# A decoder layer on eight cores: fused layer norms, a reordered retention slot, value weights loaded behind x, and a final wait for the stores alone

## The reference

```python
def layer_norm(x, w, b):
    mu = mean(x); var = mean((x - mu)**2)
    return (x - mu) * rsqrt(var + 1e-5) * w + b

hcat = x @ w_in                                  # 1024 -> 3584 columns
b_gate, c_gate, hc, q, k, v, g = split(hcat)     # 512 each
y_conv = b_gate * causal_short_conv(c_gate * hc, conv_w)    # 3 taps, per channel
q = rotary(q, positions)
k = rotary(k, positions) * 128 ** -0.5           # 4 heads of 128
o = chunkwise_retention(q, k, v)                 # chunks of 128 rows, decay per head
y_ret = silu(g) * head_group_norm(o, ret_gn_w, ret_gn_b)
mix = concat([y_conv, y_ret]) @ w_out
x = layer_norm(ALPHA * x + mix, ln1_w, ln1_b)
ff = relu(x @ w_ff1) ** 2 @ w_ff2                # 1024 -> 4096 -> 1024
ple = sigmoid(x @ w_ple_gate) * (p @ w_ple_proj)
x = layer_norm(ALPHA * x + ff + ple, ln2_w, ln2_b)
```

## Time and profile before

| what | value |
|---|---|
| median of 6 runs | 859.25 us (856.6 to 929.13) |
| profiled execution, its own time | 856.81 us |
| its span on the slowest core (core 2) | 855.3 us |
| spans of the eight cores | 850.6 to 855.3 us |
| TensorE busy | 804.4 us, 94% of the span |
| VectorE busy | 444.1 us, 52% |
| ScalarE busy | 271.5 us, 32% |
| GpSimd busy | 154.0 us, 18% |
| HBM read and written | 194.19 and 18.87 MB, 249 GB/s over the span |

### The profile page before, as it was taken

How to read it: one execution, slowest core, us unless ns; L and a number is a source line. 1 busy time by engine, 2 the same in 40 slices (tenths; PEclk the granted TensorE clock), 3 DMA queues, 4 the chain that set the end, 5 groups by cost and what they waited for, 6 DMA issues and landing times.

```text
span 855.3 us, 12652 instructions; the slowest of 8 cores (850.6 to 855.3 us)
## 1 busy us (share of the span) xinstructions
PE 804.4 (94%) x4088; PEld 375.1 (44%) x4088; DVE 444.1 (52%) x700; ACT 271.5 (32%) x496; POOL 154.0 (18%) x213
## 2 busy tenths in 40 slices
PE   3899999999979899999999999999999999999992
PEld 1344444444545344444444444444444444444441
DVE  4268745546675343635286453538555336845253
ACT  2132225554566533113144302324330222431000
POOL 7000025553455300010011000101100000100000
PEclk9999999999999999999999999999999999999996
DMA  9999999524219699999779946567976565776111
GB/s 127 219 170 156 107 168 158 88 51 99 51 19 166 164 189 195 171 174 197 185 179 243 239 122 156 140 154 215 202 217 151 146 148 170 173 204 140 52 50 49
DMA packets 22575, 128.41 MB, mean 150 GB/s; under 512 B 2864, under 2 KB 4016, under 8 KB 11056
## 3 DMA queue, kind: packets, MB, share of 16 engines
q0 software_dynamic: 13008, 81.27, 55.8%
q1 hardware_dynamic: 8928, 45.30, 15.3%
q10 hardware_dynamic: 576, 1.05, 0.3%
HBM read 194.19 MB, written 18.87 MB: 249 GB/s over the span
## 4 chain that ended last, share of the span: by engine, by line
PE 75%; DMA 8%; DVE 5%; issue 4%; POOL 4%; ACT 3%; DVEq 0%; ACTq 0%; POOLq 0%
PE ps L194 73%; DMA wc_61<-wc 4%; DMA ring_106<-w_ff 4%; ACT sqj L223 2%; PE psT L198 2%; POOL st_51 L201 1%; DVE ra_80 L201 1%; DVE ob_93 L201 1%; DVE PT_90 L201 1%; DVE ob_94 L201 0%; DVE xacc_119 L201 0%; ACT xacc_119 L223 0%; DVE PT_89 L201 0%; DVE lnst L696 0%; POOL xT_56 L236 0%
## 5 line engine op out<-in xcount | busy, mean ns | idle before, releaser
L201 DVE TENSOR_TENSOR hT<-ps,tR_129 128x512 bf16<-128x512 f32 x43 | 29.6, 688 | 30.9 <-ACT tR_129 L223 30.7
L201 POOL TENSOR_TENSOR lnst<-lnst,neghalf 128x1 f32<-128x1 f32 x32 | 19.4, 607 | 133.9 <-DVE lnst L205 133.9
L201 DVE TENSOR_TENSOR hT<-ps,tR_130 128x512 bf16<-128x512 f32 x42 | 28.9, 688 | 27.4 <-ACT tR_130 L223 27.3
L201 DVE TENSOR_TENSOR hT<-ps,tR_128 128x512 bf16<-128x512 f32 x43 | 29.6, 688 | 25.8 <-ACT tR_128 L223 25.0
L223 ACT ACTIVATE tR_128<-ps 128x512 f32<-128x512 f32 x43 | 25.7, 597 | 53.5 <-PE ps L194 49.7
L223 ACT ACTIVATE tR_129<-ps 128x512 f32<-128x512 f32 x43 | 25.6, 596 | 53.0 <-PE ps L194 47.6
L223 ACT ACTIVATE tR_130<-ps 128x512 f32<-128x512 f32 x42 | 25.1, 597 | 52.5 <-PE ps L194 51.2
L201 DVE TENSOR_TENSOR xacc_120<-ps,xacc_120 128x512 f32<-128x512 f32 x16 | 11.1, 692 | 52.1 <-PE ps L194 52.0
L194 PE MATMUL ps<-ring_110,hT 128*128 128x512 bf16 x160 | 36.2, 379 | 0.0
L194 PE MATMUL ps<-ycat,ring_106 128*128 128x512 bf16 x160 | 35.8, 379 | 0.2 <-DMA ring_106<-w_ff 0.2
L194 PE MATMUL ps<-ring_108,hT 128*128 128x512 bf16 x160 | 36.0, 379 | 0.0
(11 more groups left out here) (277 smaller groups left out, 1540.0 us busy)
## 6 DMA issues: line engine op xcount, KB each, us to landing
s_ff<-w_ff POOLq DMA_DIRECT2D x8, 1024.0 KB, 43.8
ring_106<-w_ff POOLq DMA_DIRECT2D x6, 1024.0 KB, 20.3
ring_105<-w_ff POOLq DMA_DIRECT2D x6, 1024.0 KB, 10.0
ring_110<-w_ff POOLq DMA_DIRECT2D x6, 1024.0 KB, 10.9
ring_108<-w_ff POOLq DMA_DIRECT2D x6, 1024.0 KB, 11.0
ring_109<-w_ff POOLq DMA_DIRECT2D x6, 1024.0 KB, 15.4
ring_107<-w_ff POOLq DMA_DIRECT2D x5, 1024.0 KB, 10.7
ring_104<-w_ff POOLq DMA_DIRECT2D x5, 1024.0 KB, 9.5
```

Of the source, the lines that this page charges most:

```text
L201: self.P.op(eng, lambda e: e.tensor_tensor(out=out, in0=in0, in1=in1, op=op), reads, writes)
```

## The change

The final wait of all engines for everything becomes one wait on sp for the stores (`join`). The layer norm loses its ScalarE pass and its bias step: two fused VectorE passes compute (x - mean) x weight and then x rstd + bias; epsilon is added in the same step as the aggregate, and rstd has a name of its own, so that only the second pass waits for the power. `x1_cast` is taken out of `gen_ln1` and placed by hand. In a retention slot the scores move from behind `do_rot(t, 1)` to ahead of `do_y`; in slots 9 to 12 three background steps and `do_norm` come ahead of `do_v`; slot 17 gets one more `ff1_group` ahead of `do_y`. wVf waits for xT[3] instead of wc[1]. Unit (1,0) runs alone and by piece, the units after it in a new order, and `center_v` enters after unit (2,2). ff1 makes one background step per group instead of two.

```diff
--- before.py
+++ after.py
@@ -99,21 +99,8 @@
     def dma(self, eng, fn, sem_key, reads=(), writes=()):
         return self._add(eng, fn, reads, writes, is_dma=True, sem_key=sem_key)
 
-    def join_all(self):
-        last = {}
-        dmas = {}
-        for o in self.ops:
-            if o.fn is not None:
-                last[o.eng] = o.idx
-                if o.is_dma:
-                    dmas[o.sem_key] = o.idx
-        for e in ENGS:
-            o = self._add(e, None, [], [])
-            for le, li in last.items():
-                if le != e:
-                    o.deps.setdefault(li, True)
-            for li in dmas.values():
-                o.deps.setdefault(li, True)
+    def join(self, eng, reads):
+        self._add(eng, None, reads, [])
 
     def emit(self, stack, tag):
         nc = self.nc
@@ -432,7 +419,7 @@
         for i, (t, n) in enumerate(((wG, "wG"), (wQ, "wQ"), (wK, "wK"))):
             cast(t[:], wqkvg[i], n, n)
         h.dma("sp", wVf[:], wqkvg[3].rearrange("p a (h e) -> p (a h) e", e=128), "wVf",
-              wc_res[1], ["wVf"])
+              xT_res[3], ["wVf"])
 
         wsrc = dict(wout=(w_out, s_wout), ff1=(w_ff1, s_ff1), gate=(w_gate, s_gate),
                     ff2=(w_ff2, s_ff2))
@@ -557,13 +544,12 @@
 
         conv((0, 0), by_piece=True)
         conv((0, 1), by_piece=True)
-        conv((1, 0), (1, 1), by_piece=True)
-        for tt, j in ((0, 2), (1, 2), (0, 3), (1, 3)):
+        conv((1, 0), by_piece=True)
+        for tt, j in ((1, 1), (0, 2), (1, 2), (0, 3), (1, 3), (2, 0), (2, 1), (2, 2)):
             conv((tt, j))
         bg.add(center_v())
-        for tt in (2, 3):
-            for j in range(4):
-                conv((tt, j))
+        for tt, j in ((2, 3), (3, 0), (3, 1), (3, 2), (3, 3)):
+            conv((tt, j))
         bg.flush()
         issue_casts(4)
         prefetch(3)
@@ -690,26 +676,20 @@
             st6 = lnst[:, slot, 0:12]
             mv = lnst[:, slot, 12:14]
             rstd = lnst[:, slot, 14:15]
-            nbias = lnst[:, slot, 15:16]
-            rl = ("lnst", slot)
+            rl, rr = ("lnst", slot), ("rstd", slot)
             for hf in range(2):
                 P.op("dve", lambda e, hf=hf: e.bn_stats(out=st6[:, hf * 6:(hf + 1) * 6],
                                                         in_=buf[:, hf * 512:(hf + 1) * 512]),
                      [rbuf], [rl])
                 yield
             P.op("dve", lambda e: e.bn_aggr(out=mv, in_=st6), [rl], [rl])
+            h.ts("dve", rstd, mv[:, 1:2], LN_EPS, ALU.add, [rl], [rr])
             yield
-            h.ts("dve", rstd, mv[:, 1:2], LN_EPS, ALU.add, [rl], [rl])
+            h.tt("pool", rstd, rstd, neghalf[:, 0:1], ALU.pow, [rr, "neghalf"], [rr])
             yield
-            h.tt("pool", rstd, rstd, neghalf[:, 0:1], ALU.pow, [rl, "neghalf"], [rl])
+            h.stt(buf, buf, mv[:, 0:1], w_t[:], ALU.subtract, ALU.mult, [rbuf, rl, rw], [rbuf])
             yield
-            h.stt(nbias, mv[:, 0:1], -1.0, rstd, ALU.mult, ALU.mult, [rl], [rl])
-            yield
-            h.act(buf, buf, AF.Identity, [rbuf, rl], [rbuf], scale=rstd, bias=nbias)
-            yield
-            h.tt("dve", buf, buf, w_t[:], ALU.mult, [rbuf, rw], [rbuf])
-            yield
-            h.tt("dve", buf, buf, b_t[:], ALU.add, [rbuf, rb], [rbuf])
+            h.stt(buf, buf, rstd, b_t[:], ALU.mult, ALU.add, [rbuf, rr, rb], [rbuf])
             yield
 
         def load_xin(k):
@@ -745,8 +725,9 @@
 
         def gen_ln1(tt, bi):
             yield from gen_ln(x1v(tt, bi), x1r(tt, bi), lnt[0], lnt[1], "ln1w", "ln1b", bi)
+
+        def x1_cast(tt, bi):
             h.cp("act", x1b[bi % 2][:], x1v(tt, bi), [x1r(tt, bi)], [("x1b", bi % 2)])
-            yield
 
         def x1_transpose(tt, bi):
             b = tt * 4 + bi
@@ -777,21 +758,32 @@
         slabs0 = []
         chains = []
         for t in range(NB + 2):
+            norm_first = 9 <= t <= 12
+            if norm_first:
+                bg.step(3)
+                do_norm(t - 2)
             if t < NB:
                 do_v(t)
             elif t == NB:
                 ff1_group(0, next_bank())
             bg.step()
-            if 0 <= t - 2 < NB:
+            if 0 <= t - 2 < NB and not norm_first:
                 do_norm(t - 2)
             if 0 <= t - 1 < NB:
                 do_qkT(t - 1)
+            if 10 <= t < 14:
+                bg.until(chains[t - 10])
+                x1_cast(0, t - 10)
             bg.step()
             if t < NB:
                 do_rot(t, 0)
             else:
                 ff1_group(0, next_bank())
+            if 0 <= t - 1 < NB:
+                do_scores(t - 1)
             bg.step()
+            if t > NB:
+                ff1_group(0, next_bank())
             if 0 <= t - 2 < NB:
                 do_y(t - 2)
             bg.step()
@@ -799,17 +791,13 @@
                 do_rot(t, 1)
             elif t == NB:
                 ff1_group(0, next_bank())
-            bg.step()
-            if 0 <= t - 1 < NB:
-                do_scores(t - 1)
-            bg.step()
+            bg.step(2)
             if t + 2 < NB:
                 do_g(t + 2)
             elif t <= NB:
                 ff1_group(0, next_bank())
             bg.step()
             if 10 <= t < 14:
-                bg.until(chains[t - 10])
                 x1_transpose(0, t - 10)
             if 0 <= t - 1 < NB:
                 do_o(t - 1)
@@ -852,7 +840,7 @@
         def phase_ff1(tt):
             while ff1["n"] < 32 * (tt + 1):
                 ff1_group(tt, bank3())
-                bg.step(2)
+                bg.step()
 
         scnt = [0]
 
@@ -886,6 +874,8 @@
         def gen_norm1(tt):
             for bi in range(4):
                 yield from gen_ln1(tt, bi)
+                x1_cast(tt, bi)
+                yield
                 yield
                 yield
                 x1_transpose(tt, bi)
@@ -952,13 +942,17 @@
                       [r, ("rstd", bi), "ln2b"], [r])
                 h.dma(("sp", "act")[k], out[b * 128:(b + 1) * 128, k * 512:(k + 1) * 512], v,
                       ("outl", bi, k), [r], [("out", b, k)])
+                outs.append(("out", b, k))
                 yield
+
+        outs = []
 
         def gen_out(tt, bi):
             b = tt * 4 + bi
             yield from gen_ln(x1v(tt, bi), x1r(tt, bi), lnt[2], lnt[3], "ln2w", "ln2b", 4 + bi)
             h.dma("pool", out[b * 128:(b + 1) * 128, :], x1v(tt, bi), ("outq", bi),
                   [x1r(tt, bi)], [("out", b)])
+            outs.append(("out", b))
             if tt < 2:
                 for k in ([], [0], [1], [2, 3])[bi]:
                     load_x(tt + 2, k)
@@ -978,7 +972,7 @@
             if tt < 3:
                 for bi in range(4):
                     bg.add(gen_out(tt, bi))
-        P.join_all()
+        P.join("sp", outs)
         P.emit(st, "k")
     return nc
 
```

## The result

The changed kernel takes **834.82 us** (median of 10 runs) against 858.75 us (median of 20): a ratio of 0.9725, 95% interval 0.9715 to 0.9735. The forecast was 836.2, from 830.0 to 843.5. The profiled execution of the changed kernel took 836.53 us, its span 835.0 on core 2.

A forecast was written before the change was run, and what follows sets the result against it. TensorE's own work was taken to bound the long feed-forward part, with waits in four other places. Terms 20.5 - 1.7 + 4.2 = 23.0 us, taken from the median 859.25, gave 836.2 us, range 830.0 to 843.5.

The forecast's parts named there:

- Start: Convolution start: with wVf behind x and units reordered, unit (0,2) starts at 38.7 instead of 45.19 us, 6.5 us saved.
- the slow rival (864): wVf starves behind POOL's queued transfers and lands at 113 instead of 70: 28 us lost, 864 us; chance 0.03.
- bound without any wait: Upper bound of the start's gain if TensorE did not wait at all: 6.9 us.
- Regular slots: Retention slots without a norm: scores ahead of y save 0.58 us a slot, 4.5 us up to 190.55.
- Norm slots: Four retention periods with a norm, 203.06 to 257.15 us: 54.1 us falls to 47.1, 7.0 us saved.
- With three steps and ob ahead of v: Norm slots: this VectorE order brings ob about 3.6 us later and y's turn 4.1, so periods take 12.36.
- Slot 17: Last y transposes and slab in ring_106: the load's landing moves with o(15) alone; TensorE waits 3.7 us, 1.7 us lost.
- None of this arrives: Slot 17: the 2.5 us from the added ff1 group and 0.9 in the slab are not gained, ring_106 lands late.
- bound of +5.1: Slot 17: upper bound of that term, with neither a wait for the slab nor a clock loss.
- End: Closing barrier: with the join on SP alone, POOL's DRAIN starts after its last power, span ends at 851.1, 4.2 us saved.
- The rival that the DRAIN follows the stores: Closing barrier: POOL's DRAIN ends 8 us after the stores wherever it starts, the end stays, 840.4 us; chance 0.13.
- Feed-forward: Long feed-forward part: TensorE has no gap, so the other 24 norm passes bring nothing and fewer background steps cost 0.

The follow-up runs named there:

- E4: Changed kernel with the value weights' load (wVf) waiting for the convolution weights' second piece again, not for x's third part: 845.20 us, ratio 0.9851.
- E5: Changed kernel with convolution units (1,0) and (1,1) interleaved by piece again, the value weights' load still behind x: 840.25 us, ratio 0.9802.
- E10: Kernel before with only the scores of a slot moved ahead of the y transposes: 852.25 us, ratio 0.9918.
- E9: Changed kernel with the norm's place in slots 9 to 12 undone (norm_first = False), the fused passes kept: 833.99 us, ratio 0.9723.
- E7: Changed kernel with the old layer norm (ScalarE pass, bias step, two full-width VectorE passes), its new place kept: 836.98 us, ratio 0.9751.
- E6: Changed kernel with the scores back behind the second rotated projection and after the y transposes: 849.56 us, ratio 0.9898.
- E8: Changed kernel without the added ff1 group ahead of the last y transposes in slot 17: 833.01 us, ratio 0.9719.
- E3: Changed kernel with both groups of prefetched feed-forward slabs issued one slot earlier (11 and 15, not 12 and 16): 829.06 us, ratio 0.9667.
- E1: Kernel before with only the five engines' joins replaced by one on SP that waits for the stores: 854.81 us, ratio 0.9969.
- E2: Changed kernel with the last norm's power taken off GpSimd (root on ScalarE, reciprocal on VectorE): 831.82 us, ratio 0.9702.
- E12: Changed kernel with the last norm's power off GpSimd and slabs one slot earlier, but without slot 17's added ff1 group: 828.02 us, ratio 0.9658.

## Why the prediction was right, and where it was not

**Start: right, 6.5 forecast.** (0,2) came 5.35 us earlier on core 2, o(0) 5.8 there and 6.8 by the median of the cores. xT_56 landed at 10.4 + 22.9 = 33.3 us, forecast 32.2: the 161 GB/s held (169 from 25.6 to 33.3). Both halves of the step (x alone on the queue, the bank wait gone) were needed, as it put them (E4, E5). wVf's late load cost nothing: between 39.84 and o(0) TensorE has no wait, so the slow rival (864) did not come. The prediction's bound without any wait is a slip: by its own rows 27.8 + 2 x 5.17 = 38.1, that is 7.1 earlier and not 6.9. Its other bound, a loss of 0.6 if x stays late, was too mild: E4 loses 3.1 at o(0), with the clock at 0.51 behind the wait.

**Regular slots: right.** Forecast 7 x 0.58 = 4.06, measured 4.03; the next period 0.58 (0.4 forecast), the last three 2.53 (2.1). E10 shows that the scores' place alone does this.

**Norm slots: the size right (6.5, forecast 7.0), the cause in part wrong.** That the old norm in VectorE's queue holds ob is borne out by E10's rows, and VectorE is busy 10.4 to 10.6 us of a period of 12.4 in the changed kernel, forecast 10.3. The step that failed is "With three steps and ob ahead of v, VectorE does mixing sum, statistics, ob, v": undone alone, that order costs 0.17 us (E9), and the fused passes undone alone cost 0.63 (E7). Either of the two frees ob by itself, so the order that the prediction built on was not needed. It also left out that the waits for ob and PT hide one another. With the scores late, a slot with ob in time waits for PT instead, and the changed norm brings 0.4 us in these slots and the one before (E6: 66.14 against 66.57). With the old norm, the early scores bring nothing in the four slots (E10: 54.70). Only the early scores together with a freed ob bring the 6.5.

A third edit, the cast of x1 behind the copy of q and k, is in E7 and E9 and not in E10, and the prediction has no term for its place. Of the 7.1 us between E10 and the changed kernel, 4.3 lie in the first three periods, where by E10's rows ob ends last and not the copy behind the cast. The other 2.8 lie in the fourth, where TensorE of E10 waits 2.00 us for a copy behind ScalarE's norm pass and 1.79 for one behind the cast. This split is read from the rows: the cast's place was not run by itself, nor were the fused passes and the norm's place undone together, so it is not shown by a run.

**Slot 17: the mechanism right, the size small.** "None of this arrives" held: the added group gave nothing (E8), a new wait came, and the clock fell behind it. On core 2 the wait was 4.68 us (3.7 forecast, since the slab landed 44.6 instead of 43.5 us after o(15)) and the clock's loss 2.3 (1.7). The term was -3.4 us instead of -1.7 on core 2, but -0.5 by the median of the cores: on cores 1, 3, 4 and 6 the wait was under 1.5 us and the clock stayed. The prediction took that wait as given; E3 shows that it was to be had back in full, 7.15 us on core 2. The bound of +5.1 is a slip: without wait and clock loss the term is 2.5 + 0.9 = 3.4, and 5.1 is its distance from -1.7. E3 has that 3.4 by the median of the cores (50.14 to 46.74).

**End: right, 4.2 forecast, 4.3 measured** (15.74 to 11.46), and E1 gives it alone. The rival that the DRAIN follows the stores fell twice, in E1 and E2. The Trainium skill (VectorE: DVE Perf Modes, "The DRAIN you can't avoid") puts the DRAINs around a kernel at about 12 ns on all five engines. In the kernel before, where every engine had waited in the join first, four of them agree (7, 8, 8 and 17 ns) and GpSimd does not (7,977).

**Feed-forward: right, 0.** 502.80 us before and after, on the median core.

**Sum.** 23.0 was forecast. On core 2 it was 20.3, since the slab's term was forecast 1.7 too good and the start 1.1 (5.8 at o(0) against 6.5 and 0.4); by the medians of the runs it was 23.9. That 836.2 and 834.8 lie close owes something to the norm slots, where a number worked out from the floor of 12.36 us a slot was right whichever edit removed the waits above it. Part of it is luck: the profiled execution was forecast at 833.8 and took 836.53, 2.7 us more, while the medians lie 1.4 us on the other side.

## What to carry to other kernels

Where several edits meet in one slot, the floor (the work of the bound engine) can be forecast well, but not which edit reaches it: place each edit's instruction in the queue of its engine and see who stands in front, and undo one at a time. Where one edit moves a wait, look for the next wait behind it before counting the gain. Time gained ahead of a prefetched load is lost at that load unless the transfers queued in front of it are asked for earlier too. Look at which engine's closing DRAIN ends last, and take late work off an engine whose DRAIN is long.

## What was unexpected of the hardware

GpSimd's closing DRAIN takes 8 us even when GpSimd has been idle for over 4 us. In the kernel before its last power ended at 842.77, and the DRAIN, behind the join, took 7,977 ns from 847.1. Where no join stands in front it starts with GpSimd's last own work: 8,946 and 8,952 ns with a 0.92 us power in it, 12,048 behind the issue of a slab (E2), where it hides altogether. The others are different. VectorE's takes 17 ns behind the join and 1,324 in the changed kernel, TensorE's 8 and 4,075, and these long ones end where the engine's own last instruction does (828.7 and 823.5). ScalarE's takes 8 and 153. Only GpSimd's outlasts its engine's work by microseconds here.

The same wait isn't followed by the same clock on each core: behind 2.74 us of waiting in E12, five cores lost 1.6 to 1.7 us to half clock and three nothing; behind 1.40 us on core 4 of the changed kernel nothing was lost.
